# Two up units interleaved behind gate phases, and one small copy moved, in a twelve-block decoder in fp32r parts

## What is computed

```python
def rmsnorm(x, gain):
    xf = x.astype(jnp.float32)
    y = xf * lax.rsqrt(jnp.mean(xf * xf, axis=-1, keepdims=True) + EPS)
    return (y * gain.astype(jnp.float32)).astype(x.dtype)

def swiglu(x, w_gu, w_down):
    g, u = jnp.split(x @ w_gu, 2, axis=-1)
    return (jax.nn.silu(g) * u) @ w_down

# eight times, at both places of each layer:
h = x + 0.5 * swiglu(rmsnorm(x, g[0]), w_ffn_gu[layer, 0], w_ffn_down[layer, 0])
# after the second of a layer, the gate phase:
gate = jax.nn.sigmoid(rmsnorm(h, g[3]) @ w_ple_gate[layer])
x = h + gate * (p[layer] @ w_ple_proj[layer])
```

## Time and profile before

| | |
|---|---|
| median of three runs | 2535.61 us (2531.32 to 2536.54) |
| profiled execution | 2533.78 us, its span 2532.0 us |
| VectorE busy | 72% of the span |
| ScalarE busy | 51% |
| DMA | 438 MB, mean 173 GB/s |

### The profile page before, as it was taken

One profiled execution on the slowest core, in us unless ns is written; L12 is line 12 of the kernel. 1 busy time (PEld: TensorE's weight loads), 2 busy tenths in 40 slices (PEclk: granted clock), 3 DMA queues, 4 the chain that ended last, 5 costly groups with the idle time before them and its releaser, 6 DMA issues.

```text
span 2532.0 us, 41750 instructions
## 1 busy us (share of the span) xinstructions
PE 2488.9 (98%) x17528; PEld 2272.9 (90%) x17528; DVE 1831.7 (72%) x2221; ACT 1283.4 (51%) x1449; POOL 29.3 (1%) x62
## 2 busy tenths in 40 slices
PE   8999999999999999999999999999999999999998
PEld 7889988898898988988888889888998889999998
DVE  7858778677866777688567877785867868688665
ACT  5545355445534555455465554553545545444643
POOL 0000000000000000000000000000000000011000
PEclk9999999999999999999999999999999999999999
DMA  6554335554544445445533555455425554445452
GB/s 264 200 190 177 117 138 196 203 184 167 199 174 160 146 175 200 183 168 198 200 132 121 185 203 184 173 192 195 183 85 183 190 201 163 167 144 173 145 182 83
DMA packets 62782, 438.04 MB, mean 173 GB/s; under 512 B 7536, under 2 KB 8688, under 8 KB 10640
## 3 DMA queue, kind: packets, MB, share of 16 engines
q1 hardware_dynamic: 59984, 426.95, 46.4%
q0 software_dynamic: 2624, 8.52, 1.1%
HBM read 431.25 MB, written 1.05 MB: 171 GB/s over the span
## 4 chain that ended last, share of the span: by engine, by line
PE 75%; DVE 13%; ACT 8%; issue 2%; DMA 0%; SPq 0%; ACTq 0%; DVEq 0%
PE ps L829 18%; PE ps L749 16%; PE ps L843 10%; PE ps L831 9%; DVE w_lo L1726 7%; ACT w_hi L1297 5%; PE ps L767 5%; PE ps L844 5%; PE ps L783 2%; ACT scratch L1329 1%; PE ps L846 1%; PE ps L847 1%; PE ps L848 1%; DVE scratch L1786 1%; DVE scratch L1813 1%
## 5 line engine op out<-in xcount | busy, mean ns | idle before, releaser
L1726 DVE TENSOR_TENSOR w_lo<-raw,w_hi 128x2048 fp32r<-128x2048 f32 x404 | 924.4, 2290 | 270.8 <-ACT w_hi L1297 261.4
L1297 ACT CAST w_hi<-raw 128x2048 fp32r<-128x2048 f32 x404 | 770.4, 1907 | 556.9 <-PE ps L844 216.3
L829 PE MATMUL ps<-left,w_hi 128*128 128x512 f32 x1408 | 494.6, 396 | 10.9 <-DVE left L1780 9.4
L829 PE MATMUL ps<-right,w_hi 128*128 128x512 f32 x1408 | 490.6, 395 | 0.7 <-DVE right L1780 0.7
L749 PE MATMUL ps<-right,w_hi 128*128 128x256 f32 x2272 | 422.2, 285 | 3.0 <-DVE right L2052 2.2
L831 PE MATMUL ps<-left,w_lo 128*128 128x256 f32 x1408 | 393.4, 279 | 0.0
L831 PE MATMUL ps<-right,w_lo 128*128 128x256 f32 x1408 | 390.7, 277 | 0.0
L749 PEld LDWEIGHTS ps<-right,w_hi 128*128 128x128 f32 x2272 | 357.6, 192 | 7.8 <-issue 3.1
L829 PEld LDWEIGHTS ps<-left,w_hi 128*128 128x128 f32 x1408 | 265.0, 188 | 74.0 <-issue 8.9
L749 PE MATMUL ps<-right,w_lo 128*128 128x256 f32 x1136 | 321.3, 283 | 0.0
L829 PEld LDWEIGHTS ps<-right,w_hi 128*128 128x128 f32 x1408 | 264.0, 188 | 62.7 <-DVE right L1780 1.3
(11 more groups left out here) (315 smaller groups left out, 3446.0 us busy)
## 6 DMA issues: line engine op xcount, KB each, us to landing
raw<-weights_dram SPq DMA_DIRECT2D x404, 1024.0 KB, 4.8
scratch<-scratch POOLq DMA_DIRECT2D x48, 64.0 KB, 2.0
raw<-weights_dram SPq DMA_DIRECT2D x2, 512.0 KB, 5.4
x<-x_t_dram SPq DMA_DIRECT2D x2, 512.0 KB, 6.9
scratch<-c_second_dram POOLq DMA_DIRECT2D x1, 1024.0 KB, 11.3
scratch<-p_t_dram POOLq DMA_DIRECT2D x4, 256.0 KB, 2.9
scratch<-mem_t_dram POOLq DMA_DIRECT2D x1, 1024.0 KB, 6.8
out_dram<-scratch SPq DMA_DIRECT2D x4, 256.0 KB, 2.8
```

The costliest lines, as they stand in the source:

```text
L829: nc.tensor.matmul(o, w_hi[:, w, wc], both(XG[2][:, k]), start=(k == 0), stop=False, skip_group_check=True)
L1297: nc.scalar.copy(w_hi[:, m % SPLIT, :], raw[:, m % RAW, :]).then_inc(weights_hi, 1)
L1726: V.tensor_tensor(w_lo[:, m % SPLIT, :], raw[:, m % RAW, :], w_hi[:, m % SPLIT, :].bitcast(F32), ALU.subtract).then_inc(weights_split, 1)
```

## The change

In feed-forward phases directly behind a gate phase (three of the eight) up units 0 and 1 are no longer issued one behind the other. TensorE issues chunks 0 to 5 of unit 0, chunks 0 to 5 of unit 1, chunks 6 and 7 of unit 0, chunks 6 and 7 of unit 1. The waits are the same, and each unit raises weights_used with its last matmul. In all eight phases ScalarE copies the small half of up unit 21 behind the silu of unit 20 and ahead of unit 20's cast; before, it copied it behind that cast.

```diff
@@ in ffn(i) of TensorE
-                up(0, xg_ready, parts=(i == 0))
-                up(1)
+                def first_two():
+                    for part in range(2):
+                        for j in range(2):
+                            w, e = (n0 + j) % SPLIT, e0 + j
+                            if part == 0:
+                                pe.wait_ge(weights_split, n0 + j + 1)
+                                pe.wait_ge(bank_read, e + 1)
+                            for k in range(0, KC - 2) if part == 0 else range(KC - 2, KC):
+                                if j == 0:
+                                    pe.wait_ge(xg_ready, x0 + k + 1)
+                                for half in range(2):
+                                    wc = slice(k * 256 + half * P, k * 256 + (half + 1) * P)
+                                    o = ps[:, up_bank(i, j) + half, :]
+                                    nc.tensor.matmul(o, w_hi[:, w, wc], both(XG[2][:, k]), start=(k == 0), stop=False,
+                                                     skip_group_check=True)
+                                    last = nc.tensor.matmul(o[:, T:2 * T], w_lo[:, w, wc], XG[0][:, k, :], start=False,
+                                                            stop=(k == KC - 1), skip_group_check=True)
+                            if part:
+                                last.then_inc(weights_used, 1)
+                if i and phases[i - 1][0] == "ple":
+                    first_two()
+                else:
+                    up(0, xg_ready, parts=(i == 0))
+                    up(1)
                 norm_sums(i)
                 up(2)
@@ in ffn(i) of ScalarE
                 for j in range(HCH):
-                    if j > 1:
+                    if 1 < j < HCH - 1:
                         small(j)
                     if j:
                         high(n0 + j + SPLIT)
                     gate = FFN_T[j % 2][:, 0]
                     act.wait_ge(up_scaled, h0 + j + 1)
                     nc.scalar.activation(gate, gate, ACT.Silu).then_inc(silu_ready, 1)
+                    if j == HCH - 2:
+                        small(HCH - 1)
                     act.wait_ge(hidden_value, h0 + j + 1)
                     nc.scalar.copy(hidden_parts(i, j)[:, 0], FFN_H[:, j % 2]).then_inc(hidden_hi, 1)
```

## The result

| | before | changed |
|---|---|---|
| median | 2534.69 us (20 runs) | 2539.69 us (20 runs) |
| span of the profiled execution | 2532.0 us | 2537.3 us |

The account below looks back on a forecast made before the run. TensorE was taken as the bound (98% busy), the ScalarE/VectorE chain having no slack from up unit 4 on. On 2533.78 us: 7.6 + 5.8 - 1.1 - 1.6 = +10.7, so 2544.5; median forecast 2545.5, range 2537 to 2550.

Parts of the forecast that it names:

- The stall of unit 0 goes: Up unit 0 in three phases behind gate phases: the chunk 6 stall disappears, 0.61 us gained, together 1.97 us.
- The cast comes 3.63 us later, what follows it 2.57: ScalarE's weight cast three units ahead starts 3.63 us later; w_lo, folds, rstd chain, silu and product come 2.57 us later.
- Two new waits, about 1.9 and 1.1 us, unit 4 at 26.0: TensorE waits for rstd at unit 3 and w_lo at unit 4, which starts 26.0 us after unit 0; net +7.6 us.
- The small copy, 1.6 us in four phases: First four down units behind mixers: the earlier small copy brings the fold about 1 us forward; -1.6 us in all.
- The pace, +5.8 us: From up unit 4 in three phases, 18 units at 5.66 us, not 5.55: 1.95 us a phase, +5.8 us together.
- The first down units of the three phases, -1.1 us: Behind gate phases: the slow pace removes the fold wait anyway; with it the first four down units give back 1.1 us.
- rival 1: All three phases behind gate phases keep the fast pace: +4.0 us, 2538 to 2540, within 0.2%; chance 0.13.
- the mixed case: One or two of the three phases behind gate phases keep the fast pace: +6.2 or +8.4 us; chance 0.17.
- Rival 2: VectorE's own work ahead of w_lo hides the late cast, so the change gains: -5.5 us, 2528 to 2530; chance 0.05.
- Rival 3: Clock falls to 1.2 GHz behind unit 3's wait: 1 to 2 us a phase more, 2547.5 to 2550.5; chance 0.09.

## Why the prediction was right in its mechanism and wrong in its size

- *The stall of unit 0 goes:* right, unit 0 takes 5.65 us in all three phases.
- *The cast comes 3.63 us later, what follows it 2.57:* right, 3.62 and 2.57. The run with the late cast alone shows it to be the cause, and the runs with one, three and six chunks show the cover of 1.06 us.
- *Two new waits, about 1.9 and 1.1 us, unit 4 at 26.0:* right. They are 1.76 and 0.85 us of idle time; by the unit starts units 2 and 3 take 1.9 and 1.2 us longer. Unit 4 is at 25.98 and 25.99. In the phase where the clock fell it is 26.45.
- *The small copy, 1.6 us in four phases:* right (1.6 by the profiles; with the three phases behind gate phases 2.8 by the medians).
- *The pace, +5.8 us:* this is the step that failed. I took it for all three phases, since the first phase has the same two waits and runs slow. In the first profile only the phase at 1087 us was slow (101.86 us for 18 units, the other two 99.85 and 99.95), and in the two profiles of the change two phases of six, so it is worth about 1.9 us an execution and not 5.8. I had the rows to see that it is a matter of chance (2 of 9 waits left the pace fast) and still put the whole term into the likeliest case, as if three draws would all fall on one side. I also took it that the slow pace goes away only at the sums of squares; in six phases of the twelve profiles unit 3 ran slow and the wait at unit 4 ended it, in the changed kernel at 1614.52. And the first phase is a poorer model than I made of it: the row at 29.07 in the earlier trace rows shows no idle time worth a bracket at unit 3, where the changed kernel waits 1.76 us. Over all twelve profiles, phases with a real wait at unit 3 or 4 and no further fp32 matmul ran slow in 18 of 29 cases, phases with the wait of 0.08 us of the earlier trace rows in one of six, and phases without any never.
- *The first down units of the three phases, -1.1 us:* 1.8, since fast phases still lost that wait. It belongs to the same step: at the fast pace there was more to win.
- Without the pace term, the sum is rival 1's +4.0 us; the measured 5.0 lies between that and one slow phase (+6.2), the mixed case to which I gave 0.17. The balance of the phases in the profile, +6.4, is that mixed case; what brings the span down to 5.3 lies in stretches of which the prediction said nothing, so that 5.0 came out so near to rival 1 is in part chance.
- *Rival 2* was wrong in itself. I let the change win as soon as the cast wasn't late. The run with one chunk shows that it doesn't: unit 4 starts when its w_lo is there, with the stall or without it (23.44 and 23.41). I had written that the chain has no slack at unit 4, and that sentence already rules out any gain from TensorE ahead of it.
- *Rival 3* happened in part. The clock fell behind 3 of 6 waits of 1.76 us in the changed kernel, though the earlier trace rows showed no fall behind 1.89. It cost 0.46 us a time and not 1 to 2: unit 3 took 1.7 us longer, but most of that lay beside the wait for w_lo that would have followed.

## What to carry to other kernels

Before a stall is filled on one engine, look who waits for the work that is put off: here a weight cast reused the buffer of the delayed unit, and on its engine the whole norm stood behind it. Then look at the next place where that engine meets the other chain; if it arrives there without slack, filling the stall only moves the wait, and the chain has to be shortened first (here by one reordered copy, worth some 6 us: 9.2 us below before together with the moved small copy, which alone had 2.8). Delay work by as little as the stall needs: one chunk of 0.7 us covered 0.6 us of stall, six cost 2.6.

## What the runs showed of the hardware

The same stream of fp32r matmuls of 512 and 256 columns runs at 5.55 or 5.65 us per 32 matmuls, with a granted clock of 1.00 in both (in the changed kernel 99.95 us from 1614.52 on and 101.86 us from 1112.88 on, 18 units each). A real wait can bring the slow pace (18 of 29 phases) and can end it too (six phases; in the first phase of the run with the fp32 matmul a pair takes 0.353 us in unit 3 and 0.346 behind the wait of 0.85 us at 36.37). Behind the sums of squares, an fp32 matmul, unit 2 ran at the fast pace in all 96 phases of the twelve profiles. Where one was added it met the slow pace once, and the fast one followed (0.353 us a pair before, 0.347 behind). Whether it is the fp32 matmul that does it, or any break in the stream, no run here tells apart.

The clock fell to 1.2 GHz behind 4 of 12 waits of 1.76 us and behind 3 of 3 waits of 3.13 us, all with TensorE busy through units 1 and 2 until the wait. Behind the one at 584.97 in the changed kernel it was 0.52 on average over 3.50 us and 0.99 over the next 3.30; behind the one at 587.15 with the late cast it was 0.50 over 3.50 us.
